# Attention order: the gate of a step is finished behind the rotation of q and k, and not at the beginning of the next step

## The reference

```python
h = rms_norm(x, norm_g); p = h @ w_in                 # 1024 -> 3328 columns
qa, ka, va, ga, qb, kb, vb, gb = split(p)             # 512,128,128,512 | 512,512,512,512
qa = rotary(rms_norm(qa, q_norm_g)); ka = rotary(rms_norm(ka, k_norm_g))
attn = softmax_with_sinks(qa @ ka.T / 8, window=128) @ va   # 8 q heads, 2 kv heads, 64 wide
ret  = retention(rotary(qb), rotary(kb), vb)          # 4 heads, chunks of 128, running state
x = x + concat(silu(ga) * attn, silu(gb) * rms_norm(ret)) @ w_out
```

## Time and profile before

| | |
|---|---|
| runs | 2024.65, 2032.57, 2043.05 us (median 2032.57) |
| the profiled execution's own time | 2035.98 us |
| its span in the trace | 2034.2 us |
| stage A in the trace, layer 0 | about 64 to 434 us |
| stage A in the trace, layer 1 | about 1090 to 1428 us |
| TensorE busy | 1809.1 us (89%) |
| VectorE busy | 1381.5 us (68%) |
| ScalarE busy | 721.3 us (35%) |
| GpSimd busy | 68.5 us (3%) |
| mean granted TensorE clock | 0.966 of full |

### The profile page before, as it was taken

One profiled execution on the slowest core, in us unless ns is written; L12 is line 12 of the kernel. 1 busy time (PEld: TensorE's weight loads), 2 busy tenths in 40 slices (PEclk: granted clock), 3 DMA queues, 4 the chain that ended last, 5 costly groups with the idle time before them and its releaser, 6 DMA issues.

```text
span 2034.2 us, 35760 instructions
## 1 busy us (share of the span) xinstructions
PE 1809.1 (89%) x11752; PEld 992.6 (49%) x11752; DVE 1381.5 (68%) x4712; ACT 721.3 (35%) x1809; POOL 68.5 (3%) x108
## 2 busy tenths in 40 slices
PE   0777888967999999987998979987799999999999
PEld 0344545533555555543444545554455555555444
DVE  4668888855665676677885788886576657666542
ACT  3555566621222222232442545564212221222110
POOL 3010000010000000021001000001000000000000
PEclk9799999987999999988998999999899999999999
DMA  5874444353000210079994233335310021003875
GB/s 146 190 184 84 83 94 88 78 156 95 12 10 10 97 61 10 12 188 219 246 240 132 49 68 62 77 65 138 70 50 10 10 96 61 10 10 89 205 205 155
DMA packets 353806, 196.66 MB, mean 97 GB/s; under 512 B 296624, under 2 KB 327536, under 8 KB 353552
## 3 DMA queue, kind: packets, MB, share of 16 engines
q1 hardware_dynamic: 343984, 159.89, 33.8%
q0 software_dynamic: 9728, 35.66, 5.5%
HBM read 88.75 MB, written 41.16 MB: 64 GB/s over the span
## 4 chain that ended last, share of the span: by engine, by line
PE 53%; DVE 23%; DMA 12%; issue 4%; SPq 3%; ACT 2%; DVEq 0%; ACTq 0%; POOL 0%
PE PB L514 22%; PE PA L514 21%; DMA r<-r 9%; DVE r L1016 3%; DVE r L1050 2%; DVE mix L1125 2%; PE S L668 1%; PE OB L687 1%; PE TK L657 1%; PE S L703 1%; DMA out<-r 1%; PE OB L694 1%; DVE w_mx L871 1%; DVE land L971 1%; DVE r L991 1%
## 5 line engine op out<-in xcount | busy, mean ns | idle before, releaser
L514 PE MATMUL PA<-w_a,hT 128*128 128x512 f16 (+1 forms) x1920 | 406.1, 362 | 26.5 <-DVE land L1003 26.3
L514 PE MATMUL PB<-w_a,hT 128*128 128x512 f16 (+1 forms) x1920 | 405.7, 362 | 14.2 <-DVE land L1003 13.1
L514 PEld LDWEIGHTS PA<-w_a,hT 128*128 (+1 forms) x1920 | 185.5, 99 | 201.0 <-DVE land L1003 32.9
L514 PEld LDWEIGHTS PB<-w_a,hT 128*128 (+1 forms) x1920 | 185.1, 99 | 197.2 <-DVE land L1003 19.3
L514 PE MATMUL PA<-w_b,hT 128*128 128x512 f16 x768 | 181.5, 387 | 21.6 <-DVE land L1003 21.6
L514 PE MATMUL PA<-w_b,r 128*128 128x512 f16 x768 | 174.5, 384 | 24.5 <-DMA r<-r 22.1
L514 PE MATMUL PB<-w_b,hT 128*128 128x512 f16 x768 | 181.1, 387 | 3.9 <-DVE r L1152 3.9
L1781 ACT ACTIVATE r<-OB 128x128 f32<-128x128 f32 (+1 forms) x136 | 36.4, 273 | 388.9 <-PE S L703 362.5
L1716 ACT ACTIVATE r<-r,nm,unqk 128x256 f32<-128x256 f32 x256 | 150.2, 588 | 67.8 <-DVE sd L1063 67.8
L514 PE MATMUL PB<-w_b,r 128*128 128x512 f16 x768 | 171.3, 379 | 0.0
L1172 DVE TENSOR_TENSOR r<-S,t_dec 128x256 f32<-128x256 f32 x64 | 27.2, 425 | 158.1 <-PE S L668 157.9
(11 more groups left out here) (251 smaller groups left out, 2772.0 us busy)
## 6 DMA issues: line engine op xcount, KB each, us to landing
out<-r SPq DMA_DIRECT2D x40, 512.0 KB, 4.7
r<-mixed SPq DMA_DIRECT2D x32, 512.0 KB, 4.0
w_b<-in_w_in POOLq DMA_DIRECT2D x16, 512.0 KB, 8.5
mixed<-mix SPq DMA_DIRECT2D x32, 256.0 KB, 2.0
w_a<-in_w_in POOLq DMA_DIRECT2D x16, 512.0 KB, 9.5
mixed<-mix SPq DMA_DIRECT2D x64, 128.0 KB, 1.8
w_b<-in_w_out POOLq DMA_DIRECT2D x16, 512.0 KB, 7.4
r<-in_x_prompt SPq DMA_DIRECT2D x16, 512.0 KB, 4.6
```

The lines of the kernel that those rows point to most:

```text
L514: last = nc.tensor.matmul(out[0:s.rows, 0:n], lhs, w16(ph, k, p, wpart), start=(k == 0 and part == 0 and wpart == 0), stop=(k == KT - 1 an ...
```

## The change

In stage A the gate of step s is issued at the end of VectorE's step s, directly behind the rotation of q and k and ahead of a_plo(t, 0), of the second w_low and of late_h. It was issued as the first instruction of VectorE's step s + 1. In step 1 it comes behind a_softmax(0, 1), ahead of late_h; in step 2 behind a_mix(0, 1); the gate of the last tile, E, moves from the beginning of the stretch after the loop to the end of step 16. The gate of the sample tile stays where it was. No instruction is added or taken away, and no other engine's program changes.

```diff
@@ a_first @@
                     a_rotate(L, s, ch)
                     a_softmax(L, s - 1, 1)
+                    gate("A", L, s, 2, A_W, A_W + 2 * KV_W)
@@ a_step @@
                     t, u = s - 1, s - 2
-                    gate("A", L, t, 2, A_W, A_W + 2 * KV_W)
                     if u.sample:
...
                         a_norm_link(s, ch, 11)
                         a_rotate(L, s, ch)
+                        gate("A", L, s, 2, A_W, A_W + 2 * KV_W)
                         a_plo(L, t, 0)
                         if k is not None:
                             w_low(L, "B0", k, 1)
                     else:
                         a_norm(s, ch)
                         a_rotate(L, s, ch)
                         a_mix(L, u, 1, old)
+                        gate("A", L, s, 2, A_W, A_W + 2 * KV_W)
                         a_plo(L, t, 0)
@@ layer, behind the loop @@
                 F = mid(STEPS - 1)
-                gate("A", L, E, 2, A_W, A_W + 2 * KV_W)
                 m0 = a_rr(L, E - 1, 0)
```

## The result

The changed kernel takes 2050.99 us (median of 17 runs, 2042.5 to 2055.51), the kernel before 2033.18 (17 runs beside them, 2024.65 to 2050.13). The ratio is 1.008, 95% interval 1.0062 to 1.0099, so the change costs 16 us (12.6 to 20.1). I had said 2035 with a range up to 2046. The profiled execution took 2047.07, 11.1 more than that of before, and its mean granted clock is 0.967 where it was 0.966.

The account below looks back on a forecast made before the run. VectorE's chain plus a DMA transpose, not TensorE, was taken to bound stage A. Terms 3.28 + 1.49 - 0.60 - 1.6 = +2.6 us on 2032.6 gave 2035 us, range 2026 to 2046.

Parts of the forecast that it names:

- What bounds stage A: Stage A's steady steps: VectorE's work plus a DMA transpose sets the length; TensorE's 23.8 us gate wait is off path.
- Part 1: Stage A's eight weight-converting steps per layer: gate waits for tanh, 0.27 us (layer 0) or 0.14 (layer 1); +3.28 us.
- Part 2: Stage A's other steps: 0, except in layer 0 step 2 (later transpose, +1.49 us) and step 4 (-0.60).
- step 4: Layer 0, stage A: the gate moves into VectorE's 0.83 us wait for ScalarE; -0.60 us.
- Part 3: Stage A's last tile: weight load goes ahead of the first transpose, yet TensorE's products end earlier; -0.8 us each layer.
- The rival of the falling clock: Steps where TensorE's waits change place: its clock falls, four uncovered falls +10 us, near 2045; chance 5%.
- The rival "T0 late": Stage A's end: first transpose lands late, TensorE's clock stays down; +2.5 us each layer, 2042; chance 17%.

Follow-up runs that it names:

- e2: The kernel before with only the gate of the last tile moved behind its rotation; 2042.56 us, ratio 1.0035.
- e9: The changed kernel with GpSimd's B1 weight load also waiting for the next-to-last tile's probability split, so issued behind its first transpose; 2040.74 us, ratio 1.0035.
- e1: The changed kernel with the gate of the last tile back at its old place in both layers; 2040.22 us, ratio 1.0025.
- e3: The kernel before with only the gates of steps 8 to 15 moved; 2037.28 us, ratio 1.0015.
- e4: The changed kernel with the B1 weight load held until both transposes of the next-to-last tile have landed; 2029.04 us, ratio 0.9976.
- e5: The kernel before with the B1 weight load held until both transposes of the next-to-last tile have landed; 2022.2 us, ratio 0.9943.
- e6: The kernel before with the B1 weight load held until all transposes of stage A have landed; 2025.26 us, ratio 0.9947.
- e10: As e5, with the last keys and values stored ahead of the last tile's mix and the B0 state loads; 1998.43 us, ratio 0.983.
- e13: The kernel before with only the last keys and values stored early, ahead of the last tile's mix and the state loads; 2010.13 us, ratio 0.9886.
- e11: As e6, with the last keys and values stored ahead of the last tile's mix and the state loads; 1992.85 us, ratio 0.9799.
- e8: The changed kernel with the gate one instruction later, behind a_plo(t, 0), from the third step on; 2030.9 us, ratio 0.999.
- e12: As e10, with the gate directly behind the probability split that follows the rotation, as in e8; 1998.92 us, ratio 0.9837.

## Why the prediction was wrong, point by point

**What bounds stage A: right, but for steps with a fall.** TensorE's 23.8 us of waits for the gate vanished, 21.5 us of waits for a_lo came, and no steady step got shorter. The sentence that the chain never visits TensorE had been read in layer 0; in layer 1's steps with a fall it does.

**Part 1, the hold: right in layer 0, right as a mechanism in layer 1.** Predicted 0.27 and 0.14 for each gate, measured 0.27 and 0.14. The eight steps of layer 0 grew by 0.27 to 0.35, together 2.5 where 2.16 was said; the profiles don't explain the rest. The rule that the prediction takes from the Trainium skill (page "VectorE: DVE Perf Modes", section "The DRAIN you can't avoid"), that the next instruction waits for the empty pipe, would have given 0.08 less for each. The same section adds that an instruction which isn't held starts earlier, and the rows agree with that: 279.15 against a rotation's end at 279.23. The gate's wait of 0.19 behind the rotation's end together with the lost overlap of 0.08 is what the step paid.

**Part 2: right in its mechanism**, +1.49 for T0; step 4 -0.8 where -0.6 was said. The stretch from step 2's rotation to step 3's grew by 1.99, and is 29.9 to 30.2 us in the four profiles with this order and 27.9 to 28.7 in the ten others, so the term was some 0.4 too small. From the rotation of step 2 to that of step 16 of layer 0 the parts give +3.05; measured +3.2. That they agree so well is partly luck: the hold and step 2 came out 0.4 and 0.5 dearer, and step 3, which swings between 18.6 and 19.3 us in profiles of one order, came out 0.55 shorter.

**Part 3, the last tile: wrong, and this is the step that failed.** Its sentence was: "T1 follows it, and as the engines carry the same bytes without a pause it lands at 432.8 to 433.3". The engines carried the same bytes, and in 21.3 us and not 17.5; T1 didn't follow T0 at the old distance either, since T0's issue grew from 2.24 to 4.86 us. I had taken the upper bound for T0 (16.0) from T1's row, but T1 had met the load only when T0 was through; a transpose mingled with the load from its beginning is outside both rows, 20.0 us. Two things of the part were right: T0 landed near the load's end, and the 12 products behind T1 ran at full clock (2.75 us). Measured: +2.0 and +3.5 to the last mix (in e2's profile +5.6 and +10.1) where -0.8 each was said. With e2's +7.1 us (3.9 to 10.6) and e9's return this term is shown by experiment.

The Trainium skill, page "DMA: Bandwidth & Descriptors", section "Queues, rings and completion order", says that each engine takes turns between its queues, a whole packet at a time. An even exchange is what the earlier trace rows show, and I built on it. The turns alone don't give the time: how long a packet of the load takes changed too, from 0.18 to 0.48 us in 420 to 424.

**The rival of the falling clock: right in kind, by the count of falls.** From rotation 2 to rotation 16, layer 1 takes 276.6, 279.2, 275.5, 276.5 and 275.6 us in the five profiles with the gate behind the rotation (changed, e1, e3, e4, e9), mean 276.7; 272.3, 272.1, 271.7, 273.7, 273.0, 274.3 and 271.3 in the seven with the old place (before, e2, e5, e6, e10, e13, e11), mean 272.6. That is +4.1 where part 1 had 1.1. Falls are 4, 6, 4, 4, 3 and 2, 2, 1, 3, 3, 2, 1. e8 and e12, whose gate frees the bank nearly as early but without a hold, have 273.2 and 276.7 us and 3 and 5 falls. So an early gate goes with 3 to 6 falls and a late one with 1 to 3, in 14 profiles. I gave this rival 5% and four falls of 2.5 us; by the stretches it is some two more falls of about 1.4, an estimate from (4.1 - 1.1) over 2.2 falls. That the earlier gate causes them is not shown by an experiment that changes the stand alone, and the medians don't confirm the price: e3 and e8 leave it within their uncertainty.

**The rival "T0 late"**, 2042: both halves of its condition came true, and its mechanism did not. T0's reader started at 435.4, and the granted clock was 0.50 until 439; but by 440 it was 1.00, and the 12 products behind T1 took 2.75 us and not 5.30. The loss lay in the transfers themselves. That its price of +5.0 for both layers stands near the +5.5 measured to the last mix is luck.

**The numbers.** Parts 1 and 2, +4.2, against e1's +5.1 (1.6 to 8.5); part 3, -1.6, against +7.1. Of the 14 us between the forecast of +2.6 and the measured +16, part 3 is 9 and parts 1 and 2 with the falls are 1; the other 4 are what e1 and e2 don't add up to, and they stay open. The range ended at +12 from the parts. Part 3 went over its bound of +5.0 by 2, since that bound was taken inside two rows of which neither showed the order of transfers that the change makes. By itself that would have left the median inside the range; the 4 open us took it beyond.

## What to carry to other kernels

An instruction that frees a buffer is also a trigger: ask which bulk load it releases and which small, urgent transfer stands beside it, and let the load wait for that transfer by name rather than by luck of the order. A bound taken from two rows holds only if the new order lies between theirs. And a wait of 24 us that is off the chain is worth nothing, while two transfers that changed places by less than 2 us cost seven (3.9 to 10.6).

## What the runs showed of the hardware

- Two DMA transposes and a load of 4.19 MB, the same 5312 packets, took 17.5 us when the first transpose was issued 0.74 us ahead of the load, and 21.3 us when it was issued 1.00 behind it.
- The issue of the first transpose on SyncE's queue took 2.24 us in the first case and 4.86 in the second (e2, with the second order: 7.99); the next transpose was issued behind it.
- With the load held back, the second transpose is read 9 us behind the last rotation (e4, e5) and not 20 to 33.
- The issue of two state loads on SyncE's queue took 6.5 us in e5 and 11.4 in e6, where they met the weight load.
